# A streaming encoder step on one core: the two head halves alternate inside the attention products

## Chip, cores and metric

The kernel runs on 1 core of one Trainium2 chip. The metric is the device time of one execution in microseconds (us). Three executions of the kernel before took 1833.22, 1828.02 and 1829.65 us; their median is 1829.65 us.

## What is computed

The reference is one inference step of a one-layer trunk for two groups of requests that share all weights: a new prompt of 256 rows, and 8 running streams of 16 rows each, 384 rows of width 2048 in all. Everything is in fp32. The part that the change touches is the sliding-window attention of the 16 query heads of width 64, which share 2 key/value heads (8 query heads to each):

```
def swa_sample(q, k_new, v_new, k_past, v_past, sinks):
    k = jnp.concatenate([k_past, k_new], axis=1)      # 128 cached rows + 16 new rows
    v = jnp.concatenate([v_past, v_new], axis=1)
    s = jnp.einsum('btjgd,bsjd->bjgts', q, k) * (SWA_HEAD_DIM ** -0.5)
    p = softmax_with_sink(s, sink)
    o = jnp.einsum('bjgts,bsjd->btjgd', p, v)
```

The prompt has the same attention over a band of its own rows. Around it stand: conditioning vectors times `w_ada` (six row sets that shift, scale and gate), the projection by `w_in`, a gated linear attention, the projection by `w_out`, a router, 32 experts of hidden width 512, and a final norm. The weights of all 32 experts are read once.

## The kernel before

The program is written out by hand for each engine; there is no scheduler, and TensorE runs its instructions in the order of the program. The stages are:

1. Conditioning vectors and the first columns of `w_in` (`ada_quarter`, `dense`), up to about 150 us.
2. A loop over 20 loads `n` of `w_in`, four k-chunks `kk_` each (L952 to L971). One call of `projection(n, kk_)` makes 4 products of 384 columns (L849, `n` below 12) or 3 of 512 columns (L853). Into this stream of products other work is put: at `kk_` = 1 some rows of `w_ada` (`ada`, L807), and 24 attention steps `s`, given out by `slot_step`. Steps 0 to 15 are the prompt's (a tile `t` of 128 rows and a pair of heads `m`), steps 16 to 23 are the 8 running streams, one per step.
3. The rest of the projection with the gated linear attention in between (L1095 on), which waits once for the last attention output (`o_sb` 24), then `w_out` (L1153, L1180), router and tables.
4. The experts: L1290 (gate and up), L1313 (down), whose weights come through a ring of 12 units of 1 MB in SBUF.
5. The final norm and the output.

An attention step goes through three calls on TensorE, each in a later slot of the loop: `scores(s)`, `probs_T(s)` (transposes, L919 or L923/L924) and `values(s)`. Between scores and `probs_T`, VectorE scales the scores out of PSUM (L1842 or L1849), finds the maximum, ScalarE takes the exponential (L1455), and VectorE divides by the sum (L1866). ScalarE copies the transposed probabilities (L1468, L1470/L1471) and the result (L1479, L1482).

Each step holds two **halves** `u`: rows 0 to 63 and rows 64 to 127 of the partitions (`r = slice(64 * u, 64 * u + 64)`). In `scores` of a stream, half `u` reads partitions `r` of queries and keys and writes partitions `r` of PSUM bank 4 + `u`: a 64x64 piece of the array. For each key/value head `j` there is one product over the 128 cached keys (L902, 128 columns) and one over the 16 new keys (L903, 16 columns). In `values` of a stream, both halves write to bank 4, half `u` to partitions `r`: the product over cached keys has 128 rows of contraction (L946), the one over new keys 16 (L948), 64 columns each. So a stream has 8 products in `scores` and 8 in `values`. In `values` of a prompt step there are one or two tiles of keys `kt` for each half (L941, 128 rows of contraction, 128 columns).

An fp32 product appears in the trace as two passes: one product is two LDWEIGHTS (PEld) and two MATMUL (PE) records, so that "x2" in a timeline row is one product.

The DMA queue of SyncE (SP) loads weights. `w_in` and `w_out` go through 4 units of the ring, each load waiting until the unit was used 4 loads before (L374), and the rows of `w_ada` through 4 other units (L383). Expert loads (L442) wait for the use of the same unit by the expert before, and for the first expert for the last use by `w_out`, or for the router's transposes (`h2T_ps`).

Of the kernel before, what the change touches and what calls it, by code (L numbers as in the profile page):

```python
# [20 lines left out]
P = 128  # L21
# [7 lines left out]
SWA_H, SWA_KV = 16, 2  # L29
# [73 lines left out]
def encoder_step(nc, A, O):  # L103
    with ExitStack() as ctx:  # L104
# [47 lines left out]
        bank = [ctx.enter_context(nc.psum_tensor(f"bank{i}", [P, QN], F32)) for i in range(8)]  # L152
# [16 lines left out]
        zT = zbuf[:, :].rearrange("p (k n) -> p k n", k=16)  # L169
# [27 lines left out]
        PT = dbuf[:, 3072:4096].rearrange("p (u n) -> p u n", u=2)  # L197
# [537 lines left out]
        def _(pe):  # L735
            mm, tr = nc.tensor.matmul, nc.tensor.transpose
# [3 lines left out]
            for k in range(KC):  # L740
                last = tr(bank[5][:, 9 * k:9 * k + 9], crow[:, k * P:(k + 1) * P], ident[0:9, 0:9])
# [93 lines left out]
            for k in range(KC):  # L835
                r = 32 * (k % 4)
                last = mm(bank[6][r:r + 16, 0:TOK], w[:, k, :], hT[:, k, :], start=(k < 4), stop=(k >= KC - 4))
# [40 lines left out]
            def scores(s):  # L878
                if s == 0:
                    pe.wait_ge(kT_sb, 1)  # L880
                else:
                    pe.wait_ge(sc_sb, s)
                if s == 8:
                    pe.wait_ge(ev_a, 2)
                    pe.wait_ge(ev_v, 2)
                if s >= 3:
                    pe.wait_ge(o_sb, s - 2)
                if s == 16:
                    pe.wait_ge(qs_sb, 1)
                    pe.wait_ge(past_sb, 4)  # L890
                for u in range(2):
                    out = bank[4 + u]
                    r = slice(64 * u, 64 * u + 64)
                    if s < 16:
                        t, m = STEPS[s]
                        nk = P * (t + 1)
                        last = mm(out[:, 0:nk], zT[r, m, t * P:(t + 1) * P], kT2[r, m // 4, 0:nk], start=True, stop=True)
                    else:
                        b = s - 16
                        for j in range(SWA_KV):  # L900
                            q = q_s[r, b, j, :]
                            mm(out[r, 144 * j:144 * j + 128], q, past_kT[r, b, j, :], start=True, stop=True)  # L902
                            last = mm(out[r, 144 * j + 128:144 * j + 144], q, kT2[r, j, 256 + 16 * b:272 + 16 * b],  # L903
                                      start=True, stop=True)
                last.then_inc(sc_ps, 1)

            def probs_T(s):
# [19 lines left out]
            def values(s):  # L927
                pe.wait_ge(pT_sb, s + 1)
                pe.wait_ge(sc_sb, min(s + 3, 24))
                if s:  # L930
                    pe.wait_ge(o_sb, s)
                if s == 16:
                    pe.wait_ge(vnew_in, 16)
                out = bank[4][:, 384:512]
                for u in range(2):
                    r = slice(64 * u, 64 * u + 64)
                    if s < 16:
                        t, m = STEPS[s]
                        j = m // 4
                        for kt in range(t + 1):  # L940
                            last = mm(out[r, 0:P], kva[:, kt, 128 + 64 * j:192 + 64 * j],  # L941
                                      PT[:, s % 2, (2 * u + kt) * P:(2 * u + kt + 1) * P], start=(kt == 0), stop=(kt == t))
                    else:
                        b = s - 16
                        for j in range(SWA_KV):
                            mm(out[r, 64 * j:64 * j + 64], cache_v[:, b, 64 * j:64 * j + 64],  # L946
                               PT[:, s % 2, j * P + 64 * u:j * P + 64 * u + 64], start=True, stop=False)
                            last = mm(out[r, 64 * j:64 * j + 64], v_new[:, b, 64 * j:64 * j + 64],  # L948
                                      PT[0:16, s % 2, 256 + j * P + 64 * u:256 + j * P + 64 * u + 64], start=False, stop=True)
                last.then_inc(o_ps, 1)  # L950

            for n in range(20):  # L952
                for kk_ in range(4):
                    s = slot_step(2 * n + kk_ // 2)
                    projection(n, kk_)
                    if n == 0:
                        if kk_ == 0:
                            keys_T()
                        past_T(kk_)
                    if kk_ == 1:  # L960
                        for a in range(ada_by(n), ada_by(n + 1)):
                            if a > 32 and a % KC == 0:
                                pe.wait_ge(mods, (a - 32) // KC)
                            ada(7, a)
                    if s is not None and kk_ % 2 == 0 and s < 24:
                        scores(s)
                    if s is not None and kk_ % 2 == 1:
                        if 0 <= s - 1 < 24:
                            probs_T(s - 1)
                        if 0 <= s - 2 < 24:  # L970
                            values(s - 2)  # L971
# [293 lines left out]
            for j in range(NT):  # L1265
                last = mm(bank[6][:, 0:NE], ones[:, :], rt[:, ORDER[j], 96:128], start=(j == 0), stop=(j == NT - 1))
# [1065 lines left out]
```

## Time and profile before

| | |
|---|---|
| median of three executions | 1829.65 us (1828.02 to 1833.22) |
| span of the profiled execution | 1835.3 us |
| PE busy | 1573.0 us, 86% of the span, 8925 matmuls |
| PEld (weight loads) busy | 804.1 us, 44% |
| VectorE (DVE) busy | 391.8 us, 21% |
| ScalarE (ACT) busy | 191.9 us, 10% |
| GpSimd (POOL) busy | 165.2 us, 9% |
| DMA | 616.74 MB, mean 336 GB/s |

The profile is of a fourth execution; for it only its span is given, 1835.3 us, which is 5.65 us above the median. How to read it: the shares of busy time are averages over stages with different limits. The page cuts the span into 40 slices of 45.9 us and gives a digit for each, the busy share in tenths. Matmuls are pipelined and overlap, and a record lasts from its start to a modelled end, so the times at which successive groups of records start say what a group costs TensorE; the sum of durations does not.

### The profile page before, as it was taken

To read this page: it belongs to the slowest core of one execution; us is meant where nothing else is said; L and a number is where in the kernel's file an instruction comes from. 1 tells how busy PE (TensorE), PEld (TensorE's weight loads), DVE (VectorE), ACT (ScalarE), POOL (GpSimd) and SP (SyncE) were. 2 spreads that over 40 slices of the span, in tenths; PEclk is the share of its full clock that TensorE was granted. 3 is DMA by queue.
4 is the path that set the end of the run, shared out by engine and by line. 5 is a ranking of instruction groups with operands and counts; after the bars stand their busy time and mean duration, and the time that the engine had idled before them with its cause. 6 is when DMAs were issued, how large, how long until landed. Compare 5 with 4: busy or idle time off the path is not lost. (4 is left out here: it accounts for less than half of the span.)

```text
span 1835.3 us, 21754 instructions
## 1 busy us (share of the span) xinstructions
PE 1573.0 (86%) x8925; PEld 804.1 (44%) x8925; DVE 391.8 (21%) x879; ACT 191.9 (10%) x518; POOL 165.2 (9%) x358
## 2 busy tenths in 40 slices
PE   5999999999999999978978777777778777778777
PEld 2455454444454444555534343434344434334432
DVE  2012322224242220452111111111111111111115
ACT  3001111111211100110000000000000000000002
POOL 1031000000102020020101101010101010100000
PEclk9999999999999999979989999999999999999998
DMA  9998777656626595379999999999999999999992
GB/s 364 381 308 300 287 275 298 263 221 257 205 69 234 176 229 158 154 270 424 425 427 428 427 427 427 428 428 427 427 426 422 426 426 424 422 426 422 426 389 91
DMA packets 103463, 616.74 MB, mean 336 GB/s; under 512 B 15669, under 2 KB 17829, under 8 KB 67817
## 3 DMA queue, kind: packets, MB, share of 16 engines
q1 hardware_dynamic: 85922, 571.73, 76.7%
q0 software_dynamic: 17488, 44.27, 8.0%
q8 instruction: 38, 0.62, 0.1%
q14 instruction: 15, 0.12, 0.0%
HBM read 602.50 MB, written 34.16 MB: 347 GB/s over the span
## 5 line engine op out<-in xcount | busy, mean ns | idle before, releaser
L1290 PE MATMUL bank<-ring,zbuf 128*64 128x256 f32 x4096 | 474.5, 387 | 154.2 <-DMA ring<-in_w_expert_up 96.3
L1290 PEld LDWEIGHTS bank<-ring,zbuf 128*64 128x64 f32 x4096 | 289.8, 139 | 351.1 <-DMA ring<-in_w_expert_up 120.2
L1313 PE MATMUL bank<-ring,hbuf 128*64 128x512 f32 x1024 | 237.4, 610 | 31.2 <-ACT hbuf L1662 23.0
L853 PE MATMUL bank<-ring,hbuf 128*128 128x512 f32 x384 | 174.2, 599 | 3.0 <-ACT xbuf L1440 2.6
L1313 PEld LDWEIGHTS bank<-ring,hbuf 128*64 128x64 f32 x1024 | 71.2, 140 | 176.3 <-issue 127.7
L849 PE MATMUL bank<-hbuf,ring 128*128 128x384 f32 x384 | 133.8, 495 | 1.2 <-ACT zbuf L1436 0.8
L1153 PE MATMUL bank<-ring,zbuf 128*128 128x512 f32 x288 | 128.7, 602 | 3.1 <-DVE ring L1967 1.9
L853 PEld LDWEIGHTS bank<-ring,hbuf 128*128 128x128 f32 x384 | 70.2, 190 | 83.7 <-issue 82.7
L849 PEld LDWEIGHTS bank<-hbuf,ring 128*128 128x128 f32 x384 | 69.8, 190 | 52.5 <-issue 11.0
L1153 PEld LDWEIGHTS bank<-ring,zbuf 128*128 128x128 f32 x288 | 54.3, 192 | 69.9 <-issue 69.8
L677 POOL CAST cur<-stab 128x1 int32 (+1 forms) x31 | 5.6, 180 | 831.6 <-DVE zbuf L2153 831.6
L2153 DVE COPY zbuf<-bank 128x512 f32<-128x512 f32 x31 | 21.4, 692 | 249.6 <-PE bank L1313 249.6
L2144 DVE TENSOR_SCALAR hbuf<-hbuf 128x256 f32<-128x256 f32 x32 | 9.4, 294 | 271.4 <-ACT hbuf L1639 271.4
L1273 PE MATMUL bank<-ident,zbuf 128*128 128x128 f32 x256 | 41.0, 309 | 29.0 <-DMA zbuf<-h_rows,cur 29.0
L2148 DVE TENSOR_TENSOR hbuf<-hbuf,bank 128x256 f32<-128x256 f32 x32 | 13.5, 421 | 241.3 <-PE bank L1290 241.3
L1635 ACT COPY zbuf<-bank 128x512 f32<-128x512 f32 x32 | 18.8, 586 | 386.8 <-PE bank L1273 386.8
L807 PE MATMUL bank<-ring,dbuf 128*32 128x512 f32 x512 | 59.1, 596 | 0.0
L2145 DVE RECIPROCAL hbuf<-hbuf 128x256 f32<-128x256 f32 x32 | 56.1, 1753 | 1.1
L794 PE MATMUL bank<-hbuf,ring 128*128 128x384 f32 x128 | 50.3, 516 | 3.2 <-issue 3.2
L1273 PEld LDWEIGHTS bank<-ident,zbuf 128*128 128x128 f32 x256 | 33.9, 198 | 41.5 <-DMA zbuf<-h_rows,cur 32.3
L773 PE MATMUL bank<-ring,dbuf 128*32 128x512 f32 x256 | 39.0, 685 | 5.8 <-DMA ring<-in_w_ada 4.8
L1180 PE MATMUL bank<-ring,zbuf 128*128 128x512 f32 x96 | 43.6, 612 | 0.0
(400 smaller groups left out, 1129.6 us busy)
## 6 DMA issues: line engine op xcount, KB each, us to landing
ring<-in_w_expert_up SPq DMA_DIRECT2D x64, 2048.0 KB, 26.9
ring<-in_w_expert_gate SPq DMA_DIRECT2D x64, 2048.0 KB, 26.8
ring<-in_w_expert_down SPq DMA_DIRECT2D x64, 2048.0 KB, 26.1
ring<-in_w_ada SPq DMA_DIRECT2D x96, 1024.0 KB, 7.9
ring<-in_w_in SPq DMA_DIRECT2D x32, 1024.0 KB, 9.0
ring<-in_w_out SPq DMA_DIRECT2D x16, 1024.0 KB, 6.6
y_rows<-modr POOLq DMA_DIRECT2D x1, 6144.0 KB, 22.6
ring<-y_rows SPq DMA_DIRECT2D x3, 2048.0 KB, 22.9
```

What stands on the lines that cost most here:

```text
L773: last = mm(bank[7][32 * q:32 * q + 32, :], cT[:, 4 * u + q, :], w[:, q, :], start=(u == 0), stop=(u == 3))
L794: last = mm(bank[c][:, 0:TOK], wq[:, k % 4, c * P:(c + 1) * P], hT[:, k, :], start=(k == 0), stop=(k == KC - 1))
L807: last = mm(bank[b][32 * q:32 * q + 32, :], cT[:, k, :], w[:, q * QN:(q + 1) * QN], start=(k == 0), stop=(k == KC - 1))
L849: last = mm(bank[c][:, 0:TOK], w[:, kk_, c * P:(c + 1) * P], hT[:, k, :], start=(k == 0), stop=(k == KC - 1))
L853: last = mm(bank[t][:, :], hT[:, k, t * P:(t + 1) * P], w[:, kk_, :], start=(k == 0), stop=(k == KC - 1))
L1153: last = mm(bank[3 * (b % 2) + t][:, :], zT[:, k, t * P:(t + 1) * P], w[:, i % 4, :], start=(k == 0), stop=(k == KC - 1))
L1180: last = mm(bank[3 + t][:, :], zT[:, k, t * P:(t + 1) * P], w[:, k % 4, :], start=(k == 0), stop=(k == KC - 1))
L1273: last = tr(bank[c // 4][:, (c % 4) * P:(c % 4 + 1) * P], rows[:, c, :], ident[:, :])
L1290: last = mm(bank[2 + j // 4][64 * q:64 * q + 64, 0:256], xeT[u][:, k % 8, k // 8, :], w[:, kk_, 256 * q:256 * q + 256], start=(k == 0), st ...
L1313: last = mm(bank[5 + n][64 * q:64 * q + 64, :], hidT[u][:, k % 2, k // 2, :], unit(8 + k)[:, 1024 * q + QN * n:1024 * q + QN * n + QN], st ...
L2145: link(v.reciprocal(sg[u], sg[u]))
L2153: cp(ysb[u][:, 0:QN], bank[5][:, :]).then_inc(y_v, 1)
```

## The change

In `scores` and in `values` the loop over the two halves becomes the innermost one. In `values` of a stream all four products over cached keys now come first (both `j`, both halves), then all four over new keys; before, each product over cached keys was followed by the one over new keys. As two accumulations are now open in bank 4 at once, only the first product of a half starts the bank (`start=(j == 0)`), and the last one ends it. No product is added or removed, no operand changes, and no wait or signal moves. `scores` of a prompt step has the same order as before.

```diff
-                for u in range(2):
-                    out = bank[4 + u]
-                    r = slice(64 * u, 64 * u + 64)
-                    if s < 16:
...
-                    else:
-                        b = s - 16
-                        for j in range(SWA_KV):
-                            q = q_s[r, b, j, :]
-                            mm(out[r, 144 * j:144 * j + 128], q, past_kT[r, b, j, :], start=True, stop=True)
-                            last = mm(out[r, 144 * j + 128:144 * j + 144], q, kT2[r, j, 256 + 16 * b:272 + 16 * b],
-                                      start=True, stop=True)
+                rows = (slice(0, 64), slice(64, 128))
+                if s < 16:
...
+                else:
+                    b = s - 16
+                    for j in range(SWA_KV):
+                        for u, r in enumerate(rows):
+                            mm(bank[4 + u][r, 144 * j:144 * j + 128], q_s[r, b, j, :], past_kT[r, b, j, :], start=True, stop=True)
+                        for u, r in enumerate(rows):
+                            last = mm(bank[4 + u][r, 144 * j + 128:144 * j + 144], q_s[r, b, j, :],
+                                      kT2[r, j, 256 + 16 * b:272 + 16 * b], start=True, stop=True)
...
-                for u in range(2):
-                    r = slice(64 * u, 64 * u + 64)
-                    if s < 16:
-                        t, m = STEPS[s]
-                        j = m // 4
-                        for kt in range(t + 1):
+                rows = (slice(0, 64), slice(64, 128))
+                if s < 16:
+                    t, m = STEPS[s]
+                    j = m // 4
+                    for kt in range(t + 1):
+                        for u, r in enumerate(rows):
                             last = mm(out[r, 0:P], kva[:, kt, 128 + 64 * j:192 + 64 * j],
                                       PT[:, s % 2, (2 * u + kt) * P:(2 * u + kt + 1) * P], start=(kt == 0), stop=(kt == t))
-                    else:
-                        b = s - 16
-                        for j in range(SWA_KV):
+                else:
+                    b = s - 16
+                    for j in range(SWA_KV):
+                        for u, r in enumerate(rows):
                             mm(out[r, 64 * j:64 * j + 64], cache_v[:, b, 64 * j:64 * j + 64],
-                               PT[:, s % 2, j * P + 64 * u:j * P + 64 * u + 64], start=True, stop=False)
+                               PT[:, s % 2, j * P + 64 * u:j * P + 64 * u + 64], start=(j == 0), stop=False, skip_group_check=True)
+                    for j in range(SWA_KV):
+                        for u, r in enumerate(rows):
                             last = mm(out[r, 64 * j:64 * j + 64], v_new[:, b, 64 * j:64 * j + 64],
-                                      PT[0:16, s % 2, 256 + j * P + 64 * u:256 + j * P + 64 * u + 64], start=False, stop=True)
+                                      PT[0:16, s % 2, 256 + j * P + 64 * u:256 + j * P + 64 * u + 64], start=False, stop=(j == 1),
+                                      skip_group_check=True)
```

The order of TensorE's instructions in `scores` of the first stream (step 16), before. A row is a line of the program, what it writes and reads, and the size of the output; bank4 is half 0 and bank5 half 1; L853 is the projection.

```order
L902 MATMUL bank4<-ring,xbuf 64x128
L903 MATMUL bank4<-ring,xbuf 64x16
L902 MATMUL bank4<-ring,xbuf 64x128
L903 MATMUL bank4<-ring,xbuf 64x16
L902 MATMUL bank5<-ring,xbuf 64x128
L903 MATMUL bank5<-ring,xbuf 64x16
L902 MATMUL bank5<-ring,xbuf 64x128
L903 MATMUL bank5<-ring,xbuf 64x16
L853 MATMUL bank0<-ring,hbuf 128x512
```

The same place with the change (L901 is the product over cached keys there):

```order
L901 MATMUL bank4<-ring,xbuf 64x128
L901 MATMUL bank5<-ring,xbuf 64x128
L903 MATMUL bank4<-ring,xbuf 64x16
L903 MATMUL bank5<-ring,xbuf 64x16
L901 MATMUL bank4<-ring,xbuf 64x128
L901 MATMUL bank5<-ring,xbuf 64x128
L903 MATMUL bank4<-ring,xbuf 64x16
L903 MATMUL bank5<-ring,xbuf 64x16
L853 MATMUL bank0<-ring,hbuf 128x512
```

The first product of half 1 stood behind four products of half 0, and now stands behind one. The same holds in all 8 streams.

The order in `values` of the first stream, before (L924 is the last transpose of `probs_T`, L853 the projection):

```order
L924 MATMUL bank6<-ident,ring 16x128
L946 MATMUL bank4<-dbuf,ring 64x64
L948 MATMUL bank4<-dbuf,ring 64x64
L946 MATMUL bank4<-dbuf,ring 64x64
L948 MATMUL bank4<-dbuf,ring 64x64
L946 MATMUL bank4<-dbuf,ring 64x64
L948 MATMUL bank4<-dbuf,ring 64x64
L946 MATMUL bank4<-dbuf,ring 64x64
L948 MATMUL bank4<-dbuf,ring 64x64
L853 MATMUL bank0<-ring,hbuf 128x512
```

With the change (L947 is the product over cached keys, L951 the one over new keys; x4 is four products in a row, halves 0, 1, 0, 1):

```order
L924 MATMUL bank6<-ident,ring 16x128
L947 MATMUL bank4<-dbuf,ring 64x64 x4
L951 MATMUL bank4<-dbuf,ring 64x64 x4
L853 MATMUL bank0<-ring,hbuf 128x512
```

The kind of product (128 or 16 rows of contraction) changed seven times within the call, and now changes once.

## Rows read from the trace of the kernel before

**Rows 1.** The page, 40 slices: busy tenths of PE, clock granted, DMA.

```profile
PE   5999999999999999978978777777778777778777
...
PEclk9999999999999999979989999999999999999998
DMA  9998777656626595379999999999999999999992
```

**Rows 2.** Stages: per engine busy us (records), granted clock, DMA share, GB/s.

```profile
core 0: us, PE busy (x) PEld busy (x) DVE busy (x) ACT busy (x) POOL busy (x), PEclk, DMA share, GB/s
...
340.00:475.00 135.00, 134.59 (x688) 63.22 (x678) 40.49 (x98) 18.93 (x73) 6.76 (x11) 1.00 0.66 250
475.00:640.00 165.00, 161.60 (x628) 80.74 (x629) 53.53 (x112) 30.80 (x82) 12.37 (x18) 1.00 0.49 162
640.00:790.00 150.00, 148.05 (x406) 69.14 (x405) 38.64 (x92) 12.41 (x33) 15.85 (x28) 0.98 0.58 174
790.00:830.00 40.00, 26.85 (x205) 22.16 (x206) 21.95 (x94) 5.50 (x14) 11.23 (x21) 0.70 0.93 336
830.00:1750.00 920.00, 720.97 (x5192) 383.51 (x5188) 133.08 (x187) 56.74 (x124) 85.25 (x180) 0.98 1.01 426
```

**Rows 3.** What PE waited for, 480 to 800 us: total, times, longest.

```profile
PE bank L1153 <- DVE ring L1967: 1.9, 1, 1.9
PE bank L853 <- ACT xbuf L1440: 1.2, 1, 1.2
PE bank L1153 <- ACT xbuf L1440: 1.2, 1, 1.2
PE bank L1194 <- DVE zbuf L2054: 0.7, 1, 0.7
```

**Rows 4.** What SP's queue waited for, 340 to 900 us, and its timeline.

```profile
SPq L442 <- PE bank L1180: 46.8, 1, 46.8
...
788.13 0.80 SPq L442 DMA_DIRECT2D ring<-in_w_expert_gate  x2
```

**Rows 5.** Timeline of PE, `scores` of the first stream: start us, us, records.

```profile
344.05 0.43 PE L902 MATMUL bank<-ring,xbuf 64*64 64x128 f32 x2
344.32 0.23 PE L903 MATMUL bank<-ring,xbuf 64*64 64x16 f32 x2
344.41 0.43 PE L902 MATMUL bank<-ring,xbuf 64*64 64x128 f32 x4
344.66 0.26 PE L903 MATMUL bank<-ring,xbuf 64*64 64x16 f32 x4
344.77 0.41 PE L902 MATMUL bank<-ring,xbuf 64*64 64x128 f32 x2
345.02 0.23 PE L903 MATMUL bank<-ring,xbuf 64*64 64x16 f32 x2
345.18 2.84 PE L853 MATMUL bank<-ring,hbuf 128*128 128x512 f32 x6
```

**Rows 6.** Timeline of PE, `values` of the first stream, and the last one's start.

```profile
375.54 0.33 PE L946 MATMUL bank<-dbuf,ring 128*64 128x64 f32 x2
375.80 0.32 PE L948 MATMUL bank<-dbuf,ring 16*64 16x64 f32 x2
376.05 0.33 PE L946 MATMUL bank<-dbuf,ring 128*64 128x64 f32 x2
...
377.58 1.98 PE L853 MATMUL bank<-ring,hbuf 128*128 128x512 f32 x4
...
467.12 0.33 PE L946 MATMUL bank<-dbuf,ring 128*64 128x64 f32 x2
```

**Rows 7.** PE and PEld, `values` of prompt steps: one key tile (182.68), two (348.39).

```profile
182.68 0.44 PE L941 MATMUL bank<-dbuf,kva 128*64 128x128 f32 x4
183.04 1.24 PE L849 MATMUL bank<-hbuf,ring 128*128 128x384 f32 x3
...
348.39 0.66 PE L941 MATMUL bank<-dbuf,kva 128*64 128x128 f32 x8
...
348.98 0.30 PEld L853 LDWEIGHTS bank<-ring,hbuf 128*128 128x128 f32 x2 [0.17 <-issue]
```

**Rows 8.** Lines 902 and 946 over the whole span: count, durations, first and last start.

```profile
L902 PE MATMUL bank<-ring,xbuf x64: 269/284/320, 344.1 to 436.8; 64*64 64x128 f32 x64
L946 PE MATMUL bank<-dbuf,ring x64: 222/246/271, 375.5 to 468.8; 128*64 128x64 f32 x64
```

**Rows 9.** Timelines of SP (issues) and PE (`ada`), and median landing times, 340 to 440 us.

```profile
341.41 17.66 SPq L383 DMA_DIRECT2D ring<-in_w_ada  x4
...
371.38 3.64 PE L807 MATMUL bank<-ring,dbuf 128*32 128x512 f32 x32
...
ring<-in_w_ada SPq DMA_DIRECT2D x19, 1024.0 KB, 6.7
```

**Rows 10.** DVE after the first stream's scores; PE at that stream's transposes.

```profile
348.76 0.50 DVE L1866 TENSOR_SCALAR dbuf<-dbuf,stat 128x144 f32<-128x144 f32 x2
...
358.37 0.33 PE L923 MATMUL bank<-ident,dbuf 128*128 128x128 f32 x1
```

**Rows 11.** What PE waited for, 800 to 1830 us.

```profile
PE bank L1290 <- DMA ring<-in_w_expert_up: 96.3, 52, 2.4
PE bank L1290 <- DMA ring<-in_w_expert_gate: 56.8, 47, 1.3
```

More of the change, by code:

```diff
@@ L890, in scores @@
                     pe.wait_ge(past_sb, 4)
-                for u in range(2):
-                    out = bank[4 + u]
-                    r = slice(64 * u, 64 * u + 64)
-                    if s < 16:
-                        t, m = STEPS[s]
-                        nk = P * (t + 1)
-                        last = mm(out[:, 0:nk], zT[r, m, t * P:(t + 1) * P], kT2[r, m // 4, 0:nk], start=True, stop=True)
-                    else:
-                        b = s - 16
-                        for j in range(SWA_KV):
-                            q = q_s[r, b, j, :]
-                            mm(out[r, 144 * j:144 * j + 128], q, past_kT[r, b, j, :], start=True, stop=True)
-                            last = mm(out[r, 144 * j + 128:144 * j + 144], q, kT2[r, j, 256 + 16 * b:272 + 16 * b],
-                                      start=True, stop=True)
+                rows = (slice(0, 64), slice(64, 128))
+                if s < 16:
+                    t, m = STEPS[s]
+                    nk = P * (t + 1)
+                    for u, r in enumerate(rows):
+                        last = mm(bank[4 + u][:, 0:nk], zT[r, m, t * P:(t + 1) * P], kT2[r, m // 4, 0:nk], start=True, stop=True)
+                else:
[6 more added lines that the diff above has]
+                                      kT2[r, j, 256 + 16 * b:272 + 16 * b], start=True, stop=True)
                 last.then_inc(sc_ps, 1)
@@ L934, in values @@
                 out = bank[4][:, 384:512]
-                for u in range(2):
-                    r = slice(64 * u, 64 * u + 64)
-                    if s < 16:
-                        t, m = STEPS[s]
-                        j = m // 4
-                        for kt in range(t + 1):
+                rows = (slice(0, 64), slice(64, 128))
+                if s < 16:
+                    t, m = STEPS[s]
+                    j = m // 4
+                    for kt in range(t + 1):
+                        for u, r in enumerate(rows):
                             last = mm(out[r, 0:P], kva[:, kt, 128 + 64 * j:192 + 64 * j],
                                       PT[:, s % 2, (2 * u + kt) * P:(2 * u + kt + 1) * P], start=(kt == 0), stop=(kt == t))
-                    else:
-                        b = s - 16
-                        for j in range(SWA_KV):
+                else:
+                    b = s - 16
+                    for j in range(SWA_KV):
+                        for u, r in enumerate(rows):
                             mm(out[r, 64 * j:64 * j + 64], cache_v[:, b, 64 * j:64 * j + 64],
-                               PT[:, s % 2, j * P + 64 * u:j * P + 64 * u + 64], start=True, stop=False)
+                               PT[:, s % 2, j * P + 64 * u:j * P + 64 * u + 64], start=(j == 0), stop=False, skip_group_check=True)
+                    for j in range(SWA_KV):
+                        for u, r in enumerate(rows):
                             last = mm(out[r, 64 * j:64 * j + 64], v_new[:, b, 64 * j:64 * j + 64],
-                                      PT[0:16, s % 2, 256 + j * P + 64 * u:256 + j * P + 64 * u + 64], start=False, stop=True)
+                                      PT[0:16, s % 2, 256 + j * P + 64 * u:256 + j * P + 64 * u + 64], start=False, stop=(j == 1),
+                                      skip_group_check=True)
                 last.then_inc(o_ps, 1)
```

## The prediction

> **What bounds the kernel now.** I first read the page's slices. PE stands at 9 from the second slice to the seventeenth, while the DMA line falls to between 2 and 7 in most of them; from the nineteenth slice on it is the other way round, DMA at 9 and PE at 7 [rows 1]. So there are two halves of the program with different limits, and the table by stage gives their borders. From 340 to 475 us, where the eight streams' attention lies (lines 902 and 946 start between 344.1 and 468.8 [rows 8]), PE is busy 134.59 of 135 us at full clock and DMA 66%; to 640 us 161.60 of 165, to 790 us 148.05 of 150 [rows 2]. From 830 to 1750 us DMA is full, at 426 GB/s, and PE isn't [rows 2]; there PE waits for expert weights, 96.3 and 56.8 us [rows 11].
>
> What matters then is whether time gained on PE at 340 to 475 us still exists when the expert loads begin. Between 480 and 800 us PE waits 5.0 us in all, in four waits, each for a neighbour that itself follows PE, and never for a load [rows 3]. The first expert's gate load, in turn, is held on SP for 46.8 us until `w_out` has been used, and goes out at 788.13 [rows 4]. So the stream of expert weights starts when PE says so, and a microsecond gained before 475 us is a microsecond at the end. That the later part is bound by DMA doesn't spoil this: its length stays, its start moves.
>
> **Scores of a stream.** The eight products take from 344.05 to 345.18, 1.13 us [rows 5]. The rows show three steps: at 344.05 one cached product (x2) and one new product, at 344.41 twice as many records of both lines in the same 0.43 and 0.26 us, at 344.77 again one of each. The first step is half 0 alone with head `j` = 0. In the middle step half 0 with `j` = 1 and half 1 with `j` = 0 run side by side. The last is half 1 alone. So two halves cost no more than one when both are there, but half 1 began a whole step late, with four products of half 0 ahead of it in the program. In the changed order it has one ahead. The block then has two steps, the first of 0.36 us (344.05 to 344.41) and the last with its tail of 0.41 us (344.77 to 345.18): 0.77 us, 0.36 us less. Over 8 streams that is **2.9 us**. Its bounds are 0, should half 1 be held back by something that the rows don't show, and 2.9, since each half still has its own chain of two steps.
>
> The Trainium skill speaks against this term ("TensorE: Matmul & The Clock Gate", section "Part 3: Packing small matmuls — row/col tiling"): TensorE is said to look 64 instructions ahead for weight loads that don't conflict, and to start its matmuls in strict program order. Half 1's first weight load is only 16 instructions behind the first of half 0, so by that window it overlapped already, this term is 0, and the sum below would be 10.4 instead of 13.3 us. The trace agrees with neither statement: half 1 stands idle in the first 0.36 us, and its cached product starts with the four at 344.41, ahead of half 0's new product, which is among those at 344.66 though it comes before it in the program [rows 5]. I go by the rows.
>
> **Values of a stream.** Here products of 128 rows of contraction (L946) and of 16 rows (L948) take turns, and each starts 0.255 us after the one before, whichever kind it is: 375.54, 375.80, 376.05, and so on to the projection at 377.58, 2.04 us for eight [rows 6]. For a product of 64 columns that is long. The nearest rows are the prompt's `values`: two products of 128 columns, one in each half, take 0.36 us together (182.68 to 183.04), and four, two in each half, 0.59 us (348.39 to 348.98) [rows 7]. A further product in both halves at once costs 0.23 us there, 0.115 us for half the columns. The remainder of the 0.255 us, 0.14 us, is thus paid when the kind changes: filling and emptying the array. (A check: 0.255 and 0.115 make 0.37, against the measured 0.36 for the pair of 128 columns.)
>
> After the change there are two blocks of four, one of each kind, the halves taking turns inside. A block costs 0.255 for its first pair and 0.115 for its second, 0.37 us; both 0.74 us instead of 2.04. That is 1.30 us in each stream, **10.4 us** in eight. The dear bound is a block at the price of four 128-column products, 0.59 us: 0.86 us per stream, 6.9 in all. The cheap bound is that the second pair costs nothing: two blocks at 0.255 us, 1.53 us per stream, 12.2 in all. I take 10.4, since it is built from the same kind of product in the same bank, and both halves write to bank 4 in those rows too.
>
> **Values of the prompt.** Only the 8 steps with two key tiles change their order. Four products take 0.59 us, two 0.36 [rows 7]; were they in a row, four would take about 0.36 and twice 0.23, 0.82 us. The halves run side by side already, with two products ahead of half 1. I take 0. `scores` of the prompt keeps its order: 0.
>
> **What hides what.** Nothing is added on another engine. VectorE and ScalarE get each stream's scores a little earlier, relative to the step that needs them. The room there is large: the first stream's probabilities are done at 349.26 us and `probs_T` comes to that stream after the transposes of 358.37 at the soonest [rows 10], so 9 us of room against at most 2 us gained in between. What is late next is the loads of `w_ada`. They are issued when the burst before has been used, the last of four before 359.07 us, land in 6.7 us (median), so by 365.8, and are used from 371.38 [rows 9]: room of 5.6 us between two bursts. Streams are 13 us apart (344.1 to 436.8 in seven steps [rows 8]), so two at most fall between two bursts, worth 3.3 us. I cost this at nothing; if the room were gone, the excess would come back as waits at L807.
>
> **The sum.** 2.9 + 10.4 + 0 = 13.3 us. Against the profiled execution that is 1835.3 to 1822.0 us of span. That execution lies 5.65 us above the median of the runs, and the blocks' durations don't depend on this, so the median goes from 1829.65 to **1816.4 us**.
>
> **The rivals.**
> *Only `values` gains* (the halves of `scores` overlap as far as they ever will): 10.4 us, 1819.3 us. Against it is the single step at 344.05 [rows 5]. Chance 0.09. It is also what follows from the look-ahead that the Trainium skill states.
> *Grouping helps but the halves don't overlap in the blocks*, because the two halves read the same partitions of `v_new` and the probabilities. Then a block of four is 0.255 and three times 0.115, 0.60 us; a stream saves 0.84 us, eight 6.7, with `scores` 9.6 us: 1820.0 us. The prompt's rows speak against it for the cached kind, nothing for the 16-row kind. Chance 0.08.
> *Absorbed*: the transfers of `w_ada`, or another one after 475 us, become what PE waits for, and nothing is left: 1829.7 us. For it speaks a DMA share of 66% with bursts [rows 2]; against it 5.6 us of room [rows 9]. Chance 0.08.
> *Slower*: a change of half costs the array what a change of kind costs, so that every product pays in full. The change adds 6 changes of half in each stream's `scores`, 6 in its `values`, and 2 in each of the 8 two-tile prompt steps, 112 in all. At the full price `values` of a stream stays at 2.04 us. In `scores` a cached product is then 0.36 us [rows 7] and a new one, with 48 columns fewer than 64, 0.17, four pairs 2.12 instead of 1.13: 7.9 us over eight streams. Four products at 0.36 instead of 0.59 us are 6.8 us over eight prompt steps. Sum 14.7 us, 1844.3 us. It decides from 0.06 us per change of half on, since grouping alone saves 6.7 us over 112. Against it: the pair at 182.68 is such a change of half and takes 0.36 us with both products [rows 7]. Chance 0.05.
> *That the order isn't what the source says* can be ruled out: the program's order on TensorE is written out, and shows the four-and-four blocks.
>
> **How the numbers follow.** The forecast has 0.70. Its own terms reach from 6.9 to 15.1 us (`values` 6.9 to 12.2, `scores` 0 to 2.9), 1822.8 to 1814.5 us. The runs of before spread from 1.6 us below their median to 3.6 above, and the granted clock outside the attention (0.98 and 0.70 [rows 2]) can shift by a microsecond or two. I give 1812.5 to 1824.0 us, which takes in the first two rivals and leaves out the other two, 0.13, and some 0.04 beside. Below 0.3% (5.5 us) a measurement of this kernel can't tell a change from none. Faster by more: 0.70, 0.09 and 0.08, together 0.87. Within 0.3%: 0.08. Slower: 0.05.
>
> **What the profile afterwards would show.** `scores` of a stream: two groups of x4 records 0.36 us apart and the projection 0.77 us after the first; one that still takes 1.13 us makes the first term wrong. `values` of a stream: eight records of the cached kind, eight of the new kind 0.37 us later, and the projection 0.74 us after the start; a block of 0.6 us makes it the second rival. `values` of two-tile prompt steps still 0.59 us; more means that changes of half cost. The last `values` of a stream would start about 12.0 us before 467.12 [rows 6] (all but its own 1.3 us gained by then), and the first gate load would be issued some 13 us before 788.13 [rows 4]. Waits of L807 or L853 for DMA would show the absorption. The forecast is wrong if the blocks shrink as said and the span doesn't.

## The result and the profile after

| | before | after |
|---|---|---|
| median of 8 executions each | 1830.68 us (1828.02 to 1835.99) | 1820.27 us (1818.90 to 1823.86) |
| span of the profiled execution | 1835.3 us | 1822.0 us |
| PE busy | 1573.0 us | 1559.5 us |

The ratio is 0.9937, with a 95% interval of 0.9922 to 0.9953: by it 11.5 us less, 8.6 to 14.3; the two medians themselves lie 10.4 us apart. (The forecast was made against the median of the first three executions, 1829.65 us.) The same kernel was compared once more later, with 6 executions against 17 of the kernel before: ratio 0.9930 (0.9917 to 0.9944), 12.8 us. A span is not the time of an execution: the profiled execution of the kernel after took 1823.54 us and has a span of 1822.0, and in the other executions the span is shorter by 1.5 to 1.7 us as well. So the profiled execution of the kernel before, with its span of 1835.3 us, lies some 7 us above the median of 1829.65 and not the 5.65 us given above.

The page of the kernel after, the lines that answer to [rows 1]:

```profile
PE   5999999999999999978788777777877777778777
...
PEclk8999999999999999979999999999999999999998
DMA  9998777667527593399999999999999999999992
```

The stages, in the borders of [rows 2] (the work in each has moved forward by up to 13 us):

```profile
340.00:475.00 135.00, 133.44 (x716) 58.72 (x709) 42.88 (x101) 25.25 (x85) 8.20 (x12) 1.00 0.75 280
475.00:640.00 165.00, 162.58 (x649) 81.06 (x649) 56.16 (x120) 24.24 (x71) 13.94 (x20) 1.00 0.47 154
640.00:790.00 150.00, 144.57 (x442) 72.50 (x438) 43.10 (x117) 16.73 (x43) 15.41 (x28) 0.98 0.60 189
```

DMA's share in the attention rises from 0.66 to 0.75, as the same loads fall into less time. PE stays the engine that bounds the stage, busy 133.44 of 135 us. What it misses is mostly a wait of 1.4 us for ScalarE at L853, which before came just after 475 us and now falls inside the stretch. The timeline of PE around the first stream's `scores` (start us, us, records), against [rows 5]:

```profile
344.07 0.44 PE L901 MATMUL bank<-ring,xbuf 64*64 64x128 f32 x4
344.34 0.24 PE L903 MATMUL bank<-ring,xbuf 64*64 64x16 f32 x4
344.43 0.41 PE L901 MATMUL bank<-ring,xbuf 64*64 64x128 f32 x4
344.68 0.24 PE L903 MATMUL bank<-ring,xbuf 64*64 64x16 f32 x4
344.85 2.84 PE L853 MATMUL bank<-ring,hbuf 128*128 128x512 f32 x6
```

Two steps instead of three, each with the records of both halves, and the projection (L853) 0.78 us after the first product instead of 1.13. The same for the first stream's `values` and for the last one's, against [rows 6]:

```profile
374.49 0.45 PE L947 MATMUL bank<-dbuf,ring 128*64 128x64 f32 x8
374.87 0.45 PE L951 MATMUL bank<-dbuf,ring 16*64 16x64 f32 x8
375.24 2.84 PE L853 MATMUL bank<-ring,hbuf 128*128 128x512 f32 x6
...
455.48 0.45 PE L947 MATMUL bank<-dbuf,ring 128*64 128x64 f32 x8
```

Two blocks of 0.38 and 0.37 us instead of eight of 0.255. The last one starts 11.64 us earlier than before (467.12) and is itself 1.29 us shorter: 12.93 us. And SP's queue, against [rows 4]:

```profile
775.20 0.80 SPq L442 DMA_DIRECT2D ring<-in_w_expert_gate  x2
```

The first expert's gate load goes out 12.93 us before its old time of 788.13, so in this pair of traces nothing of the gain was lost on the 320 us between. What PE waited for between 480 and 788 us is what it was in [rows 3], down to the last tenth:

```profile
PE bank L1157 <- DVE ring L1971: 1.9, 1, 1.9
PE bank L853 <- ACT xbuf L1444: 1.2, 1, 1.2
PE bank L1157 <- ACT xbuf L1444: 1.2, 1, 1.2
PE bank L1198 <- DVE zbuf L2058: 0.7, 1, 0.7
```

### The profile page after: what moved, and what is told of

It reads as the page before. It is cut to its first block and busy times, and to the rows that moved or that the text cites. A ratio compares the mean times of both kernels' runs of the same rounds, so it can differ in the third digit from the quotient of the medians.

```text
span 1822.0 us, 21754 instructions
## 1 busy us (share of the span) xinstructions
PE 1559.5 (86%) x8925; PEld 794.6 (44%) x8925; DVE 391.9 (22%) x879; ACT 191.7 (11%) x518; POOL 165.2 (9%) x358
## 5 line engine op out<-in xcount | busy, mean ns | idle before, releaser
L853 PE MATMUL bank<-ring,hbuf 128*128 128x512 f32 x384 | 174.2, 599 | 3.1 <-ACT xbuf L1444 2.6
L1157 PE MATMUL bank<-ring,zbuf 128*128 128x512 f32 x288 | 128.7, 602 | 3.1 <-DVE ring L1971 1.9
L853 PEld LDWEIGHTS bank<-ring,hbuf 128*128 128x128 f32 x384 | 70.2, 190 | 83.9 <-issue 83.0
L1157 PEld LDWEIGHTS bank<-ring,zbuf 128*128 128x128 f32 x288 | 54.3, 192 | 69.9 <-issue 69.8
L1639 ACT COPY zbuf<-bank 128x512 f32<-128x512 f32 x32 | 18.8, 586 | 386.7 <-PE bank L1277 386.7
L807 PE MATMUL bank<-ring,dbuf 128*32 128x512 f32 x512 | 59.1, 596 | 0.0
L1652 ACT COPY zbuf<-bank 128x512 f32<-128x512 f32 x31 | 18.2, 586 | 242.9 <-PE bank L1317 242.9
```

What stands on the lines that cost most here:

```text
L807: last = mm(bank[b][32 * q:32 * q + 32, :], cT[:, k, :], w[:, q * QN:(q + 1) * QN], start=(k == 0), stop=(k == KC - 1))
L853: last = mm(bank[t][:, :], hT[:, k, t * P:(t + 1) * P], w[:, kk_, :], start=(k == 0), stop=(k == KC - 1))
L1639: cp(xeT[u][:, 4:8, :, :].rearrange("p c q s -> p (c q s)"), bank[1][:, :]).then_inc(eT_a, 1)
```

## The experiments

All start from the changed kernel or from the one before; "call" is all that one stream issues in `scores` or `values`, from its first record to the projection's. Theory A is the reading in the prediction. Theory B, the rival, is that taking turns between the halves is what pays, wherever it is done.

### Each part alone

`e1_scores_only` takes `scores` from the change and `values` from before, `e2_values_only` the other way round.

```diff
-                for u in range(2):                                 # values, in e2 alone (scores as before)
+                    for j in range(SWA_KV):                        # scores, in e1 alone (values as before)
+                        for u, r in enumerate(rows):
```

> The order of scores from the change, values as in the kernel before. Theory A (half 1 waited for its turn in scores; in values the changes of kind cost): scores of a stream 0.775 us, values of a stream 2.05 us, and two-tile prompt values 0.59 us; the first expert gate load leaves SP 2.8 us earlier than before (785.3 us), the time falls by 2.8 us. Theory B (taking turns between the halves is what pays wherever it is done, and the order of the kinds hardly matters): scores carries about half of the whole gain, 5 to 6 us, if not in its own block then by what it hides around it.

> The order of values from the change, scores as in the kernel before. Theory A: values of a stream 0.76 us instead of 2.05, scores 1.13 us; the first gate load leaves SP 10.1 us earlier than before (778.0 us), the time falls by 10 us. If the two parts are independent, this and the kernel with scores alone add up to the 12.9 us that the whole change gained by that load. Theory B: 5 to 6 us.

A call of `scores` and one of `values` take 0.775 and 2.05 us with scores alone, 1.13 and 0.76 us with values alone, as theory A says. From the first stream's first score to the last stream's first value it is 123.07 us before, 120.23 with scores alone, 114.24 with values alone and 111.41 with both. With the last call's own 1.29 us, the parts save 2.84 and 10.12 us, and both together 12.95: they add up. Theory B's even split is wrong. But the times say something else. Ratios: scores alone 0.9995 (0.9983 to 1.0006), values alone 0.9923 (0.9905 to 0.9942). The second alone did what both did. So both were repeated.

> The kernel with the change in scores alone once more: 2.85 us are gone from its attention in the trace, but the first comparison gave a ratio of 0.9995 (0.9983 to 1.0006), 0.9 us. If the 2.85 us reach the end, the ratio is 0.9984; if they are lost on the way, 1.000. The half-speed stretches that come and go (1.7 us each) make single executions differ by more than that.

> The kernel with the change in values alone once more. Its attention is 10.1 us shorter in the trace. If only that reaches the end, the ratio is 0.9945; if, as the two comparisons of the scores alone suggest, the scores bring nothing and the values all that the whole change brings, it is 0.993.

Scores alone: 1.0002 (0.9990 to 1.0014), again nothing to be seen, and the expected 0.9984 is outside; it was just inside the first interval. Values alone: 0.9944 (0.9926 to 0.9963), 10.3 us. The gate loads missed their forecasts too: they left SP at 782.52 and 774.74 us, not at 785.3 and 778.0. Part of what becomes of scores' 2.84 us is seen in the traces, once the kernel before has a second one too.

> The kernel before, profiled a second time. The blocks of the kernel with scores alone are 2.85 us shorter, but its two comparisons show about nothing. One reading: the first profile of the kernel before caught an execution above the median with two half-speed stretches of 3.4 us between the attention and the experts (1.7 us each), and what the scores save is hidden by where such stretches fall. Then this trace has the same blocks (1.13 and 2.05 us), the same time from the first scores to the last values (123.07 us), and a different set of half-speed stretches; if it has the same two, the loss must be sought in the experts' part.

All eight traces side by side, in us from the start of the span; the last two columns are the granted clock of two stretches, of which the profile of after has, as an example, these rows (fields as in [rows 2]):

```profile
640.00:665.00 25.00, 23.15 (x57) 10.17 (x54) 5.62 (x10) 2.17 (x6) 11.77 (x22) 0.93 0.99 265
755.00:785.00 30.00, 29.19 (x155) 20.01 (x154) 18.33 (x57) 8.31 (x19) 0.54 (x1) 0.94 0.38 154
```

and values alone these:

```profile
640.00:665.00 25.00, 23.15 (x60) 10.26 (x60) 7.19 (x14) 2.17 (x6) 11.81 (x22) 1.00 0.87 249
755.00:785.00 30.00, 29.19 (x166) 20.68 (x165) 19.30 (x58) 8.31 (x19) 0.93 (x2) 1.00 0.42 168
```

| kernel | first score | last values | first gate load | span | 640-665 | 755-785 |
|---|---|---|---|---|---|---|
| before | 344.05 | 467.12 | 788.13 | 1835.3 | 0.93 | 0.94 |
| before, again | 342.26 | 465.33 | 784.43 | 1831.7 | 0.93 | 1.00 |
| scores alone | 343.07 | 463.31 | 782.52 | 1830.8 | 0.93 | 1.00 |
| scores alone, again | 343.15 | 463.38 | 782.58 | 1830.4 | 0.93 | 1.00 |
| values alone | 344.21 | 458.45 | 774.74 | 1822.9 | 1.00 | 1.00 |
| values alone, again | 343.14 | 457.37 | 773.67 | 1821.3 | 1.00 | 1.00 |
| after | 344.07 | 455.48 | 775.20 | 1822.0 | 0.93 | 0.94 |
| after, again | 344.46 | 455.87 | 775.55 | 1822.6 | 0.93 | 0.94 |

A granted clock below 1.00 in these columns is one stretch of 3.4 us at half speed (1.2 instead of 2.4 GHz), which takes away 1.7 us: 0.07 of 25 us, 0.06 of 30. Take from the time between last values and gate load the last call itself (2.05 or 0.76 us), and what is left is 318.96, 317.05, 317.16, 317.15, 315.53, 315.54, 318.96 and 318.93 us, down the table. With two such stretches it is 318.9 to 319.0, with one 317.1 to 317.2 and with none 315.5: each costs 1.5 to 1.9 us, and hardly anything else differs. Values alone has none in both its traces, the whole change two in both, scores alone one, the kernel before two and then one. So the whole change leaves the attention 2.8 us ahead of values alone and loses 3.4 us on the way to the experts.

Against the second trace of before, whose 1831.7 us of span are nearer to the medians, scores alone is 1.9 us ahead at the gate load, 0.8 us of a slower start taken off its 2.84, and 0.9 to 1.3 us at the end. The rest of the program adds its own spread: from the gate load to the end the eight traces take 1046.8 to 1048.2 us, and the first score starts anywhere from 342.26 to 344.46 us.

Where the half-speed stretches come from can be narrowed down with the traces of the later experiments, 14 in all. Within a trace, all moments at which the clock falls or rises in mid-program fit one even grid, to 0.01 us, and the grid lies differently against the program from one execution to the next. TensorE has a wait of 1.85 us for VectorE in the `w_out` stage (L1153 before, L1157 after), the longest between attention and experts. Where a moment of the grid lies between 0.37 us before and 0.36 us after the end of this wait, there is one stretch (five traces: before again, both of scores alone, `e6_two_ahead` and `e9_one_kind`). Where it lies 0.54 to 1.30 us after, there are two (six: before, both of the change, `e3`, `e4` and `e7`), and where it lies 1.42 to 1.73 us after, none (three: both of values alone, and `e5_three_ahead`). From the end of the wait to the gate load it is 130.7 to 130.9 us, 132.6 and 129.2 us accordingly. This sorts all 14 traces without an exception, though it does not show why. The order of the products then matters only through when the program comes to this point: the two traces of before have one and the same order and fall into different groups (1.30 us after, 0.37 before). A few microseconds gained earlier can thus move a kernel from one group to another, which is worth up to 3.4 us either way. The executions without a profile fit this without proving it: their mean granted clock is 0.978 with values alone (10 executions), 0.976 before (54), 0.976 with scores alone (22) and 0.975 with the change (14). Why scores alone shows next to nothing in the median stays open.

### Which of the two does it in values

`e3_grouped_halves_apart` keeps the two blocks but puts both products of half 0 before both of half 1. `e4_alternated_not_grouped` keeps the turns but undoes the grouping.

```diff
+ e3: for u, r in enumerate(rows):            # cached block; new block likewise
+         for j in range(SWA_KV):
+ e4: for j in range(SWA_KV):
+         for u, r in enumerate(rows): ...    # cached
+         for u, r in enumerate(rows): ...    # new
```

> As the change, but in values of a stream each block of four has both products of half 0 first, then both of half 1. Theory A: half 1 stands only two products behind, as in the prompt's values before, so the halves still run side by side: a block 0.38 us, a call 0.76 to 0.77 us, and the time is that of the change (within 0.1 us at the first gate load, 775.2). Theory B: without taking turns a block is 0.255 + 3 x 0.115 = 0.60 us, a call 1.20 us, and the first gate load leaves 3.5 us later than with the change.

> As the change, but values of a stream go by head: cached products of both halves, new ones of both halves, then the same for the second head, so the halves take turns and the kind changes three times inside the call instead of once. Theory A: each pair of a kind is 0.26 us (0.255 and a few ns for the second half), a call four pairs, 1.05 us, 0.29 us more than with the change; the first gate load 2.3 us later than with it (777.5). Theory B: no more than the change's 0.76 us.

Measured: with the halves apart 0.771 us per call against 0.759, where theory B had 1.20; with turns but without grouping 1.05, where it had no more than 0.76. Counted from the first score, the gate load comes 0.05 us later than with the change with the halves apart, and 2.1 us later (2.3 expected) without grouping. The timeline of the latter, PE:

```profile
373.66 0.34 PE L947 MATMUL bank<-dbuf,ring 128*64 128x64 f32 x4
373.92 0.33 PE L950 MATMUL bank<-dbuf,ring 16*64 16x64 f32 x4
374.18 0.34 PE L947 MATMUL bank<-dbuf,ring 128*64 128x64 f32 x4
374.45 0.33 PE L950 MATMUL bank<-dbuf,ring 16*64 16x64 f32 x4
374.71 2.84 PE L853 MATMUL bank<-ring,hbuf 128*128 128x512 f32 x6
```

Each kind starts 0.26 us after the other, now with two products inside instead of one: the price belongs to the change of kind, and the second half rides along for nothing. Turns alone thus bring 1.00 of the 1.29 us, since they put two products of a kind next to each other and leave three changes of seven; grouping alone brings 1.28. The two are not parts of a sum but two ways to the same end. By the rates of the prediction, six changes of 0.14 us less are 0.84 us of a call; the remaining 0.45 of the 1.29 us is that half 1 works beside half 0, and no longer after its four products (an estimate, as no run has one without the other). Innermost turns are worth 0.012 us a call once the products are grouped, 0.1 us in all. The times agree: halves apart 0.9928 (0.9907 to 0.9950), not grouped 0.9957 (0.9940 to 0.9974).

### Change of kind, or waiting for PSUM

Before the change each product over new keys added to what the product just ahead of it had written, so the 0.255 us could also be the wait for that result (theory D). `e9_one_kind` leaves out the new keys' part in `values` and counts the cached part twice, in the order of before:

```diff
-  last = mm(out[...], v_new[:, b, ...], PT[0:16, ...], start=False, stop=True)
+  last = mm(out[...], cache_v[:, b, ...], PT[:, ...], start=False, stop=True)
```

> The kernel before, in which the product over new keys in values of a stream is replaced by the product over cached keys once more: the same order, the same accumulation right behind on the same place in PSUM, but 128 rows of contraction everywhere. The new keys' part is left out and the cached part counted twice. Theory A (the change of kind costs 0.14 us): no change of kind inside the call, so 0.255 us for the first product, 0.115 for each of the three others of a half, and half 1, four products behind, starts when half 0's third product does, some 0.22 us later: 0.80 to 0.85 us instead of 2.05. Theory D (the second product waits for the first one's result in PSUM, since both add to the same place): pairs still start 0.255 us apart, and the call takes 1.0 us or more, up to 2.05 us.

```profile
374.62 0.33 PE L946 MATMUL bank<-dbuf,ring 128*64 128x64 f32 x2
374.78 0.28 PE L948 MATMUL bank<-dbuf,ring 128*64 128x64 f32 x2
374.90 0.34 PE L946 MATMUL bank<-dbuf,ring 128*64 128x64 f32 x4
375.02 0.34 PE L948 MATMUL bank<-dbuf,ring 128*64 128x64 f32 x4
375.19 0.28 PE L946 MATMUL bank<-dbuf,ring 128*64 128x64 f32 x2
375.31 0.28 PE L948 MATMUL bank<-dbuf,ring 128*64 128x64 f32 x2
375.52 0.70 PE L853 MATMUL bank<-ring,hbuf 128*128 128x512 f32 x1
```

The call is 0.90 us instead of 2.05. The same accumulation on the same place costs 0.12 to 0.17 us per product once both have 128 rows of contraction. Theory D is out. The picture is that of `scores` before: half 1 comes in at 374.90, together with half 0's third product. That is 0.28 us late and not the 0.22 expected, so the call misses the expected 0.80 to 0.85 by 0.05.

### How far ahead the second half is seen

> As the change, but in scores of a stream three products of half 0 stand ahead of half 1's first (half 0: cached, new, cached; half 1: the same three; then the last new product of each). In the trace of before, half 1 began when half 0's third product began, with four ahead, and at once with two ahead in the prompt's values; the rows fit a reach of some two products. Theory A (a short reach): half 1's first matmul starts when half 0's second product starts, 0.27 us after half 0's first, and the call takes 0.775 + 0.27 = 1.05 us. Theory C (a fixed delay when the halves are far apart, or half 1 waits for the first head to be done): either 0.775 or 1.13 us.

> As the change, but in scores of a stream two products of half 0 (cached and new of the first head) stand ahead of half 1's first. Theory A (a reach of two products): half 1 starts at once, the call takes 0.775 to 0.79 us, as with the change. Theory B (only strict turns let the halves run side by side): more than 0.9 us.

```diff
+ # (new, j, u), e5: three products of half 0 ahead; e6: two
+ e5: (0,0,0), (1,0,0), (0,1,0), (0,0,1), (1,0,1), (0,1,1), (1,1,0), (1,1,1)
+ e6: (0,0,0), (1,0,0), (0,0,1), (1,0,1), (0,1,0), (1,1,0), (0,1,1), (1,1,1)
```

With three ahead, PE (L905 is the cached product here, L902 the new one):

```profile
343.35 0.43 PE L905 MATMUL bank<-ring,xbuf 64*64 64x128 f32 x2
343.62 0.18 PE L902 MATMUL bank<-ring,xbuf 64*64 64x16 f32 x1
343.63 0.32 PE L905 MATMUL bank<-ring,xbuf 64*64 64x128 f32 x1
343.65 0.21 PE L902 MATMUL bank<-ring,xbuf 64*64 64x16 f32 x1
343.71 0.41 PE L905 MATMUL bank<-ring,xbuf 64*64 64x128 f32 x3
...
344.40 2.84 PE L853 MATMUL bank<-ring,hbuf 128*128 128x512 f32 x6
```

The records don't name the half. Read by the order of the program, half 1's first cached product (343.63) starts just behind half 0's second product (343.62), and the call takes 1.04 us in all eight streams, 1.05 expected. With two ahead it takes 0.795 us. So the table by the number of products of half 0 in front of half 1's first is 0.775 us for one, 0.795 for two, 1.04 for three and 1.13 for four. Neither a fixed delay (theory C) nor strict turns (theory B) give that. The third product in front is the one that hurts.

### The same idea one stage later

The gated linear attention has the same pattern (L1022 with L1025, and L1053). `e7_gla_grouped` adds to the change:

```diff
 # within, tiles 0 and 1
-for h in range(GH): full product; then for l, w: for r: small products
+for h in range(GH): full product
+for l, w in ((1, 16), (2, 32), (3, 64)):
+    for h in range(GH): for r: small products
 # outputs, tile 2
-for hh in range(2): full product; then 8 products 32 wide
+for hh in range(2): full product, start=(hh == 0)
+for hh in range(2): 8 products 32 wide
```

> The change, and the same idea in the gated linear attention: within (L1022 and L1025 of the kernel before) makes all four heads' products of one shape before those of the next, and outputs of the third tile makes both heads' full products first, then all sixteen 32-wide ones. Theory A: in within, changes of kind fall from 12 to 3 for each of two tiles, 9 x 0.14 = 1.3 us of 3.97, and with the heads' short products side by side about 2.3 us are left; in outputs one pair of changes less in each of two calls, 3.58 to 3.3 us. Together 3.3 + 0.6 = 3.9 us at the first gate load, 4 us in the time. Theory B (taking turns pays, not the kind): nothing, since each of these already goes round its pieces of the array.

The timeline of PE in the first tile of `within`:

```profile
490.20 1.05 PE L1026 MATMUL bank<-ring 128*128 128x128 f32 x8
491.18 1.30 PE L1031 MATMUL bank<-ring 128*16 128x16 f32 x56
492.41 1.13 PE L853 MATMUL bank<-ring,hbuf 128*128 128x512 f32 x2
```

From the first weight load (489.77) to the projection's it is 2.64 us instead of 3.97. Together with `outputs` the first gate load of the experts leaves at 771.01, 4.2 us before that of the change; 0.8 us of this is an earlier start, so counted from the first score the gain is 3.4 us, against 3.9 expected. The median is 1819.29 us (1814.46 to 1823.13), the ratio to the kernel before 0.9918 (0.9901 to 0.9936), the lowest of all kernels here, though its interval overlaps that of the change. The profiled execution, the slowest of the six (1823.13 us), kept next to nothing of this, with 1821.6 us of span. The granted clock around the router's tables, in that kernel and in the one with the change alone (fields as in [rows 2]):

```profile
775.00:806.00 31.00, 20.92 (x125) 18.49 (x126) 15.54 (x64) 3.80 (x8) 11.26 (x21) 0.56 0.91 330
```

```profile
775.00:806.00 31.00, 18.88 (x147) 17.48 (x145) 14.73 (x60) 6.11 (x15) 11.23 (x21) 0.75 0.89 348
```

At 0.56 instead of 0.75 some 3 us more are lost there: the products of the router's tables begin at 790.05 us against 791.08, 1.0 us ahead and no longer 4.2. Then PE waits 4.2 us for the second expert's rows, a wait that the change does not have:

```profile
PE bank L1283 <- DMA zbuf<-h_rows,cur: 4.2, 1, 4.2
```

Whether that wait belongs to the kernel or to this execution was not tried; that the change brings a gain in time here is not shown.

### The change again

> The changed kernel once more, beside the kernel before on the same chip. The trace says 12.9 us at the end of the attention, while the medians of the first comparison said 10.4. If all of it reaches the end, the ratio is 0.9930 (12.9 of 1832 us) and lies in the interval; if part of it is lost after the attention in most executions, it is nearer 0.995.

0.9930 (0.9917 to 0.9944): 12.8 us, the 12.9 of the trace. The 11.5 us of the first comparison differ from it by less than either interval.

## Why the prediction was right

**The bound.** PE sets the time at which the expert stream begins: confirmed to 0.01 us in the first pair of traces, where the 12.93 us at the end of the attention are 12.93 at the gate load. That is so since both traces have two half-speed stretches. The stream keeps its length less exactly: 1047.2 us from the gate load to the end before and 1046.8 after, so the 12.93 us became 13.3, and up to 1048.2 us in the other traces of the two parts.

**Scores, 2.9 us.** The mechanism and the size hold inside the attention: two steps, 0.775 us, 0.77 predicted, 2.84 us in all. Half 1 was late because too much of half 0 stood ahead, and the reach is two products. In the device time the term can't be seen: scores alone give 0.9995 and 1.0002. This is the weak step of the forecast, "a microsecond gained before 475 us is a microsecond at the end". It holds between traces with the same half-speed stretches; these cost 1.5 to 1.9 us each, and their number changes with the moment at which the program comes to the wait in `w_out`. The forecast had them as "a microsecond or two" of spread, which is too little beside a term of 2.9 us.

**The look-ahead.** The look-ahead of 64 instructions that the Trainium skill states ("TensorE: Matmul & The Clock Gate", "Part 3: Packing small matmuls — row/col tiling") would leave the term at 0 and make the calls of `scores` equally long in any of the orders tried. They were 1.13, 1.04, 0.795 and 0.775 us. In the time, though, the rival built on it came out as close as the forecast, for another reason.

**Values, 10.4 us.** 10.12 us. A call took 0.759 us, 0.74 predicted; a block is 0.38 instead of 0.37, since a further pair costs 0.12, not 0.115. One call of the eight took 1.00 us: in the third stream the projection now starts 0.2 us late behind its wait for the evictions at L846, which it used to find done, the only wait the change brought before the experts ("PE bank L853 <- issue: 0.2" among the waits). The bounds, 6.9 and 12.2, were far wider than needed.

**Prompt values, 0.** 0.587 against 0.594 us for two key tiles, under 0.06 us in all.

**The sum.** 13.3 predicted against the profiled execution, 13.3 measured there. That this agrees to the tenth is luck: the two traces happen to have the same start (344.05 and 344.07 us) and two half-speed stretches each. The second traces of the two kernels are 9.1 us of span apart (1831.7 and 1822.6), the other two pairings 9.7 and 12.7. In the time it is 11.5 and 12.8 us by the ratios. The time of 1816.4 us was 3.9 below the median, 1.0 us of that because three executions had put the old median 1.0 too low. The other 2.9 us are within the spread of the executions, and they are also what the term for scores was worth; the medians can't tell the two apart. The forecast came out right above all because its larger term, 10.4 us for values, is real and reaches the end. The profiled execution of before lay high, at 1835.3 us of span against 1831.7 in its second trace.

**The rivals.** *Only values gains*: wrong in the attention, right within the interval in the time, where its 1819.3 us lie nearer to the median of 1820.27 than the forecast's 1816.4. *Halves don't overlap in the blocks*: wrong, 0.38 against 0.60 us. *Absorbed by loads*: wrong, L807 never waited for DMA. *A change of half costs what a change of kind costs*: wrong; 112 of them were added and no call got longer.

## What to carry to other kernels

Where small products of different shapes take turns on TensorE, group them by shape: each change cost 0.14 us here, more than such a product itself, and it is seen in the timeline as equal spacing whatever the size. Where two parts of the array can work side by side, put no more than two products of one in front of the first of the other; strict turns bring next to nothing beyond that. And before a gain of 2 to 3 us in a kernel of 1800 is believed or given up, compare where the clock was at half speed in both traces, and take more than one trace of each: here two executions of the same kernel differed by 3.6 us of span.

## What was not expected of the hardware

- The reach for the second half is short and sharp. At three products ahead, half 1 started 0.01 us after half 0's second product; at four, with its third (0.36 us late in `scores`, 0.28 in the one-kind kernel).
- Ahead of the prediction it is said that TensorE runs its instructions in the order of the program. Between different pieces of the array this does not hold to the last: with three ahead, a cached product that stands behind half 0's second product starts (343.63) before the second pass of that product (343.65). Read as half 1's first, with half 0's own next cached product following at 343.71, it overtakes by 0.02 us.
- Between attention and experts the granted clock fell to half for 3.4 us twice, once or not at all, and each time cost 1.5 to 1.9 us. Which of the three it is goes by a shift of a microsecond between the program and the moments at which the clock changes. In the stretch of the first fall PE was busy 23.15 of 25 us; it had waited 1.9 us for VectorE at L1153 shortly before. Values alone had the same wait (1.85 us) and the same 23.15 us, and no fall. In the stretch of the second, PE was busy 30.00 of 30 us in both traces of the kernel before, and the clock fell in one of them.
